# All low parts of the mixer's weights and rows on VectorE, between the HGRN levels

## The reference, cut to what matters

```
h = h + hybrid_mixer(rms_norm(h, norm1_g[layer]), w_in[layer], ..., w_out[layer], lb)
h = h + expert_choice_ffn(rms_norm(h, norm2_g[layer]), w_router[layer], ...)

def hybrid_mixer(xn, w_in, ret_g, hgrn_g, w_out, lb):
    proj = xn @ w_in                      # (256, 1024) @ (1024, 9*512)
    rq, rk, rv, rg, hq, hf_fwd, hf_bwd, hi, hg = jnp.split(proj, splits, axis=-1)
    r_out = retention, forward and backward, normalised, * silu(rg)
    h_out = HGRN2 scan, forward and backward, normalised, * silu(hg)
    return jnp.concatenate([r_out, h_out], axis=-1) @ w_out
```

## Time and profile before

| | |
|---|---|
| median of three runs | 2313.32 us |
| the profiled execution: span from first to last instruction | 2314.5 us |
| TensorE busy | 1928.7 us (83%) |
| VectorE busy | 816.0 us (35%) |
| ScalarE busy | 605.9 us (26%) |
| GpSimd busy | 170.2 us (7%), of that 120.7 us in 26 low halves |
| mean granted TensorE clock | 0.883 of full speed |

### The profile page before, as it was taken

One profiled execution on the slowest core, in us unless ns is written; L12 is line 12 of the kernel. 1 busy time (PEld: TensorE's weight loads), 2 busy tenths in 40 slices (PEclk: granted clock), 3 DMA queues, 4 the chain that ended last, 5 costly groups with the idle time before them and its releaser, 6 DMA issues.

```text
span 2314.5 us, 26791 instructions
## 1 busy us (share of the span) xinstructions
PE 1928.7 (83%) x10580; PEld 1227.7 (53%) x10580; DVE 816.0 (35%) x1196; ACT 605.9 (26%) x850; POOL 170.2 (7%) x70
## 2 busy tenths in 40 slices
PE   6897887777777789788767777766999999987998
PEld 5876532222232587654222222235888887445887
DVE  6566200000000556630000000046454455564776
ACT  5523211101111452312111111135222122253433
POOL 1333000000000132300000000021000000010000
PEclk9998887777777799888788888888999999998999
DMA  7373999999999636389999999941322224302551
GB/s 265 110 254 112 345 375 410 410 410 410 409 410 410 229 136 219 145 309 382 410 410 409 410 410 409 410 185 37 109 74 107 108 73 148 116 27 106 184 182 55
DMA packets 184534, 585.99 MB, mean 253 GB/s; under 512 B 6688, under 2 KB 7840, under 8 KB 184224
## 3 DMA queue, kind: packets, MB, share of 16 engines
q1 hardware_dynamic: 183152, 579.89, 65.0%
q0 software_dynamic: 896, 3.67, 0.4%
q10 hardware_dynamic: 432, 1.70, 0.2%
HBM read 584.19 MB, written 1.05 MB: 253 GB/s over the span
## 4 chain that ended last, share of the span: by engine, by line
PE 56%; DMA 17%; SPq 13%; DVE 7%; ACT 5%; issue 2%; POOL 1%; DVEq 0%; ACTq 0%; POOLq 0%
DMA ring<-in_w_down 16%; SPq L2189 11%; PE bank L461 10%; PE bank L463 10%; PE bank L462 10%; PE bank L791 3%; PE bank L778 3%; PE bank L809 3%; PE bank L819 3%; PE bank L940 2%; PE bank L619 2%; PE bank L473 2%; SPq L2195 2%; PE bank L1031 1%; ACT w_high L376 1%
## 5 line engine op out<-in xcount | busy, mean ns | idle before, releaser
L791 PE MATMUL bank<-ring,xeT 128*32 128x512 f32 x2048 | 280.9, 698 | 77.8 <-DMA ring<-in_w_up 58.7
L809 PE MATMUL bank<-ring,hid_T 128*32 128x512 f32 x1024 | 201.5, 930 | 81.2 <-DMA ring<-in_w_down 69.6
L791 PEld LDWEIGHTS bank<-ring,xeT 128*32 128x32 f32 x2048 | 69.3, 121 | 250.2 <-issue 160.5
L461 PE MATMUL bank<-x_high,w_high 128*128 128x512 f32 (+1 forms) x512 | 174.7, 341 | 17.0 <-DVE x_low L376 12.0
L376 POOL TENSOR_TENSOR w_low<-ring,w_high 128x2048 fp32r<-128x2048 f32 x26 | 120.7, 4643 | 821.6 <-ACT w_high L376 819.8
L463 PE MATMUL bank<-x_high,w_low 128*128 128x512 f32 (+1 forms) x512 | 175.4, 343 | 0.0
L462 PE MATMUL bank<-x_low,w_high 128*128 128x512 f32 (+1 forms) x512 | 173.7, 339 | 0.0
L1842 DVE TENSOR_TENSOR w_low<-ring,w_high 128x1024 fp32r<-128x1024 f32 x128 | 152.9, 1232 | 36.0 <-ACT w_high L1298 32.7
L1298 ACT ACTIVATE w_high<-ring 128x1024 fp32r<-128x1024 f32 x128 | 127.3, 1050 | 142.6 <-DMA ring<-in_w_mlp_in 64.0
L461 PE MATMUL bank<-w_high,hid_high 128*128 128x512 f32 x384 | 150.4, 392 | 0.0
L462 PE MATMUL bank<-w_low,hid_high 128*128 128x512 f32 x384 | 150.4, 392 | 0.0
(11 more groups left out here) (229 smaller groups left out, 2925.1 us busy)
## 6 DMA issues: line engine op xcount, KB each, us to landing
ring<-in_w_gate SPq DMA_DIRECT2D x128, 1024.0 KB, 18.5
ring<-in_w_up SPq DMA_DIRECT2D x128, 1024.0 KB, 18.6
ring<-in_w_down SPq DMA_DIRECT2D x64, 2048.0 KB, 22.4
ring<-in_w_ada SPq DMA_DIRECT2D x24, 2048.0 KB, 8.2
ring<-in_w_in SPq DMA_DIRECT2D x18, 2048.0 KB, 10.0
ring<-in_w_mlp_in SPq DMA_DIRECT2D x16, 2048.0 KB, 8.6
ring<-in_w_mlp_out SPq DMA_DIRECT2D x16, 2048.0 KB, 7.7
ring<-in_w_out SPq DMA_DIRECT2D x4, 2048.0 KB, 9.2
```

Of the source, the lines that this page charges most:

```text
L461: mm(ps, lh, rh, start=first, stop=False, skip_group_check=True)
L791: ins = mm(psum[4][32 * g:32 * g + 32, :], xeT[:, 2 * n + k, :], w[:, k, :, 256 * g:256 * (g + 1)], start=n == 0 and k == 0, stop=n == 3 a ...
L809: ins = mm(psum[5 + half][32 * g:32 * g + 32, :], hidT[:, n, 32 * g:32 * g + 32], w[:, g, half * 512:(half + 1) * 512], start=n == 0, stop ...
```

## The change

GpSimd forms no low part any more. VectorE forms all: the second half of item 0 and the two chunks of rows at the start of the layer in its own sequence, both halves of item 5 ahead of the HGRN levels, one half behind each of the first two units of RV (halves of item 6), HI (item 7), RG (item 8) and HG (item 9), and both halves of item 10 behind the last unit. The high parts on ScalarE are moved forward: item 7 from behind HI to behind the ADA ahead of it, item 8 from behind RG to behind the ADAs ahead of it, item 9 one ADA earlier, item 10 to just behind the last row tile of HG. The semaphores of the two engines become one. GpSimd keeps a memset, transfers, and its work in the second block.

```diff
--- before.py
+++ after.py
@@ -88,12 +88,7 @@
 
 
 SPLIT = [n for n, kind in enumerate(mixer_items()) if kind != ADA]
-SPLITS, BY_VECTOR = len(SPLIT) + 2, 5
-
-
-HALVES = [(j, half) for j in range(SPLITS) for half in range(2)]
-VECTOR_HALVES = [(j, half) for j, half in HALVES if j < BY_VECTOR and (j, half) != (0, 1)]
-POOL_HALVES = [x for x in HALVES if x not in VECTOR_HALVES]
+SPLITS = len(SPLIT) + 2
 
 
 def build_program(nc, x, cols, w_in, w_out, w_router, w_gate, w_up, w_down, final_g, ctx_x, w_ada,
@@ -390,16 +385,11 @@
 
             self.then_inc(read_by[name][0], 1, read_by[name][1])
 
-    def low_item(subtract, eng, l, j):
-
-        by, halves = (("split_by_pool", POOL_HALVES) if eng is nc.gpsimd
-                      else ("split_by_vector", VECTOR_HALVES))
-        for half in range(2):
-            if (j, half) not in halves:
-                continue
-            eng.wait_ge(S_("mix_high_ready"), 2 * (SPLITS * l + j) + half + 1)
-            whole, high, low = split_half(l, j, half)
-            subtract(low, whole, high.bitcast(F32), ALU.subtract).then_inc(S_(by), 1)
+    def low_half(subtract, eng, l, j, half):
+
+        eng.wait_ge(S_("mix_high_ready"), 2 * (SPLITS * l + j) + half + 1)
+        whole, high, low = split_half(l, j, half)
+        subtract(low, whole, high.bitcast(F32), ALU.subtract).then_inc(S_("mix_low_ready"), 1)
 
     def low_chunks(subtract, b):
 
@@ -500,18 +490,9 @@
 
                 if conversion is not None and c % 2 == 0:
                     b = c // 2
-                    if conversion:
-                        pe.wait_ge(S_("mix_x_split"), 6 * l + 2 + b + 1)
-                    elif b % 2 == 0:
-                        pe.wait_ge(S_("mix_x_split"), 6 * l + b // 2 + 1)
-                    else:
-                        pe.wait_ge(S_("mix_x_split_by_pool"), 2 * l + b // 2 + 1)
-                if c % 4:
-                    return
-                for by, halves in (("vector", VECTOR_HALVES), ("pool", POOL_HALVES)):
-                    if (j, c // 4) in halves:
-                        pe.wait_ge(S_("split_by_" + by),
-                                   len(halves) * l + halves.index((j, c // 4)) + 1)
+                    pe.wait_ge(S_("mix_x_split"), 8 * l + 4 * conversion + b + 1)
+                if c % 4 == 0:
+                    pe.wait_ge(S_("mix_low_ready"), 2 * (SPLITS * l + j) + c // 4 + 1)
 
             def split_parts(j):
 
@@ -1184,6 +1165,8 @@
                         ps = full(act, name)
                         func = ACT.Silu if kind in (RG, HG) else ACT.Copy
                         free(f(where[kind][:, t, :], ps[:, :], func), name)
+                        if (kind, t) == (HG, NT - 1):
+                            high_item(l, SPLITS - 1)
                         for _ in range(2):
                             if units[u][0] == P:
                                 name = ("unit", l, u)
@@ -1193,9 +1176,9 @@
                                        ACT.Copy), name)
                             u += 1
 
-                if n > 5 and n + 3 in SPLIT:
-                    high_item(l, SPLIT.index(n + 3))
-                if n == SPLIT[-1] - 1:
+                if n > 4 and n + 4 in SPLIT:
+                    high_item(l, SPLIT.index(n + 4))
+                if n + 4 == len(mixer_items()):
                     high_item(l, SPLITS - 2)
                 if kind == HG:
                     for t in range(NT):
@@ -1216,7 +1199,6 @@
             def mix_gain(c):
                 return C("ret_g", H4 * l + c) if c < H4 else C("hgrn_g", H4 * l + c - H4)
 
-            high_item(l, SPLITS - 1)
             high_chunks(("mix", l), mix_gain)
 
 
@@ -1474,9 +1456,9 @@
                         tick(ins)
                 free(ins, (tag, b))
 
-        def split_chunks(tag, gain):
-
-            for b in (0, 1, 2, 3) if tag[0] == "mix" else (0, 2):
+        def split_chunks(tag, gain, after=lambda b: None):
+
+            for b in range(4):
                 if b % 2 == 0:
                     ps = full(dve, (tag, b))
                     for c in (2 * b, 2 * b + 1):
@@ -1491,6 +1473,7 @@
                 else:
                     freed(dve, (tag, b))
                 low_chunks(tt, b).then_inc(S_("mix_x_split"), 1)
+                after(b)
 
         def lower_bounds():
 
@@ -1520,13 +1503,22 @@
 
         for l in range(DEPTH):
 
+            def low_item(j):
+                for half in range(2):
+                    low_half(tt, dve, l, j, half)
+
             for t in range(NT):
                 normalise(1, lambda _: h[:, t, :], lambda _: xs[:, t, :], "xs_ready", first=t)
-            low_item(tt, dve, l, 0)
+            low_half(tt, dve, l, 0, 0)
             if l == 0:
                 dve.wait_ge(S_("cols"), 16)
-            split_chunks(("x1", l), lambda c: C("norm1_g", KC * l + c))
-            low_item(tt, dve, l, 1)
+
+            def second_half(b):
+                if b == 1:
+                    low_half(tt, dve, l, 0, 1)
+
+            split_chunks(("x1", l), lambda c: C("norm1_g", KC * l + c), second_half)
+            low_item(1)
             if l == 0:
                 lower_bounds()
 
@@ -1550,8 +1542,9 @@
                     free(ins, name)
                     tt(rot[:, i, t, :], rope_t[:, 0, :], rope_t[:, 1, :],
                        ALU.add).then_inc(S_("rot_ready"), 1)
-                low_item(tt, dve, l, 2 + i)
-            low_item(tt, dve, l, 4)
+                low_item(2 + i)
+            low_item(4)
+            low_item(5)
 
             expect("forget_ready", 2)
             tt(hx[:, 0, :, :], hk[:, 0, :, :], hk[:, 1, :, :],
@@ -1648,17 +1641,22 @@
                 if 1 <= u <= 2 * len(LEVELS):
                     merge(u - 1)
 
+            next_item = 6
             for kind in mixer_items()[5:]:
                 if kind == ADA:
                     if ada_n:
                         ada_bias(ada_n - 1)
                     ada_n += 1
                 else:
-                    for _ in range(4):
+                    for part in range(4):
                         one_unit(u)
                         u += 1
+                        if part < 2:
+                            low_half(tt, dve, l, next_item, part)
+                    next_item += 1
                 if kind == HG:
 
+                    low_item(SPLITS - 1)
                     for t in range(NT):
                         expect("ret_sq_ready")
                         ins = reduce(rstat[:, 0, t, :],
@@ -2054,16 +2052,8 @@
         g.memset(eps[:, :], EPS).then_inc(S_("scattered"), 1)
         g.memset(cT[:, :, :], 0.0).then_inc(S_("ones_ready"), 1)
         for l in range(DEPTH):
-            low_item(turn(g.tensor_tensor), g, l, 0)
-            for b in (1, 3):
-                freed(pool, (("x1", l), b))
-                low_chunks(turn(g.tensor_tensor), b).then_inc(S_("mix_x_split_by_pool"), 1)
-            low_item(turn(g.tensor_tensor), g, l, BY_VECTOR)
-
             freed(pool, ("ret_s", l, H4 - 1))
             g.memset(kdec[:, :, :, :], 0.0).then_inc(S_("kdec_ready"), 1)
-            for j in range(BY_VECTOR + 1, SPLITS):
-                low_item(turn(g.tensor_tensor), g, l, j)
             freed(pool, ("w_out", l, 0, 0))
             g.dma_start(wr[:, :, :], w_router[l].rearrange("(c p) e -> p c e", p=P)).then_inc(
                 S_("router_landed"), 16)
```

## The result

The changed kernel takes 2343.51 us (median of 4 runs, 2335.95 to 2345.46); the kernel before took 2314.53 beside it (2312.31 to 2318.74). The ratio is 1.012, 95% interval 1.0099 to 1.014: it is slower by 29 us, where 12.4 had been forecast and 2334 was the upper end of the range.

A forecast was written before the change was run, and what follows sets the result against it. The prediction took TensorE's path through the two mixers as the bound, mixer delays lengthening the whole. Its terms summed to +6.2 us a layer, +12.4 for both: 2313.3 + 12.4 = 2325.7, say 2326 us, range 2314 to 2334.

The forecast's parts named there:

- Start and RV: Layer start to the end of the ADA behind RV: shorter VectorE instructions and TensorE waits, -0.2 and -5.9 us a layer.
- HI: Middle of HI: new 6.3 us TensorE wait for unit 5 behind the tile's landing, plus 2.7 us slow clock, +9.5 a layer.
- RG: Middle of RG, item 8: landing 8.9 us, TensorE wait 7.1 us, slow clock behind it, +10.3 us a layer.
- the bounds: Landing of 7.8 to 10.7 us instead of 8.1 and 8.9: -0.3 - 1.1 or +2.6 + 1.8 us a layer.
- HG: HG to the end of hgrn_out: 3.0 us wait before unit 13 without clock loss, stretched instructions gone, -3.9 us a layer.
- rival 3: HG's 3.0 us wait and the start's short wait also throttle: +2.7 and up to +1 us a layer, about 2332 us; chance 0.13.
- Normalisation: Normalisation: the second ret_gate falls from 4.33 to 0.69 us on the path to the transposes, -3.6 us a layer.
- Behind the mixers: Everything behind the second mixer: no change forecast, 0 us.
- Rival 2: Mixers: tiles there in time, HI and RG cost 0, only GpSimd's removal counts: -17 us a layer, 2279 us; chance 0.07.

The follow-up runs named there:

- second profile: The changed kernel run once more, unchanged: 2340.55 us, ratio 1.0111.
- filled waits: Changed kernel with extra matmuls nobody reads, worked off by TensorE before its waits for units 5, 9 and 13: 2332.74 us; on another bank 2327.4 us.
- 2283 and 2281: Changed kernel, low halves of items 7, 8, 9 behind third and fourth unit: 2282.75 us; that with item 10's high part behind hgrn_off: 2280.77 us.
- four kernels: Changed kernel, low halves later: items 7 to 9 behind fourth unit 2288.18 us, behind third and fourth 2282.75; only item 9 2321.45, only 7 and 8 2299.97.
- half tiles: Changed kernel loading only the first 512 of 1024 rows of RG's and HG's weight tiles: 2326.18 us, ratio 1.0059.
- subtraction and memset: Kernel with low halves behind third and fourth unit, plus one GpSimd subtraction in the normalisation: 2284.58 us; with two GpSimd memsets instead: 2282.44 us.
- the kernels of 2288 and 2283 us: Changed kernel with low halves of items 7, 8, 9 behind the fourth unit: 2288.18 us; behind the third and fourth unit: 2282.75 us.

## Why the prediction was wrong

The direction was right, and so was the mechanism of HI and RG; in HG the prediction left the clock out, and its sum was less than half of what was measured. By its own steps:

- *Start and RV*, -6.1: right, -5.4, though two misses partly cancel in it: the start gave about -0.7, not -0.2, and RV -4.7, not -5.9. The short wait keeps part of the gain back: behind the 2.10 us wait at 109.95 the clock was down and the ADA of RV took 3.6 us, not 1.92.
- *HI*, +9.5: right, +10.1. Landing 7.8 us for 8.1 taken, wait 6.18 for 6.3, unit 5 and the start of the row tile at half clock. (The 0.67 of the earlier trace rows for 110 to 111 is a mean: the clock was not "back at full" there but came back within that microsecond.)
- *RG*, +10.3: mechanism right, a term too small. "I take 8.9 us to landing": the transfer requested at 149.82 took 10.6 us and the wait was 8.91, not 7.1; in the second layer the wait was 7.89; +11.9. The end of the earlier trace rows that I kept for the bounds was the case in the first layer.
- *HG*, -3.9: this is the step that failed. "A wait of 3.0 us that I take as too short to let the clock fall": the wait was 2.81 and 3.58 us (2.70 and 3.54 in the second profile), but behind it the clock was at half. Stretches of the changed kernel in HG, first layer:

```profile
195.00:197.00 2.00, 0.00 (x0) 0.00 (x0) 1.93 (x3) 1.69 (x3) 0.00 (x0) 1.00 0.51 186
197.00:199.00 2.00, 1.62 (x8) 1.62 (x8) 1.83 (x4) 0.00 (x0) 0.00 (x0) 0.55 0.00 0
201.00:203.00 2.00, 2.00 (x6) 1.61 (x6) 1.93 (x3) 0.00 (x0) 0.00 (x0) 0.50 0.00 0
205.00:207.00 2.00, 2.00 (x10) 1.62 (x9) 0.71 (x2) 0.00 (x0) 0.00 (x0) 1.00 0.00 0
```

  The clock was still full in the idle 195 to 197 and fell (1.2 GHz) as unit 13 began: 0.55 over 197 to 199 leaves 0.2 us at full, and the unit began at 197.38. The unit took 3.4 us to the start of the row tile, and the row tile 6.9 to 8.0 in the four changed mixers, where 1.8 and 5.7 are full clock. It cost 3.3 us a layer by the filled waits. I had inferred the harmless 3.0 us from one row, the 2.08 us wait before unit 0, whose own unit ran at full clock but behind which the clock was already going down, as rival 3 said. With 3.3 us more in each layer the forecast would have been 2332 us; the changed kernel is still 8 to 11 us above that, by RG's landing (3 us in both layers), smaller misses in the other steps and, in the first profile, the 6.4 us behind the mixers. The part of rival 3 on HG was the true case, and its 2332 us had the same landing too short.
- *Normalisation*, -3.6: right, -3.6, and by the cause given: ret_gate is 0.69 us and the earlier trace rows had 4.33.
- *Behind the mixers*, 0: +6.4 in one profile, +0.1 in the other, the clock again. The range had no term for waits that move the clock where the change touches nothing.

The whole account of a layer, from the experiments: the waits themselves (with the 0.4 us before units 7 and 11) cost 7.9 (HI 26.3 - 18.4), 9.1 (RG 27.5 - 18.4) and 3.4 (HG 28.4 - 25.0), 20.4 us; the clock 8.3; given back are 5.4 up to A, 6.9 in HG (31.9 - 25.0), 3.6 and 0.6, 16.5 us. That leaves 12.2, against the 12.1 measured; the terms come from the same table, so it shows that nothing is missing, not that each is right. Rival 2 named what would have happened with the tiles there in time (-17 a layer, 2279 us): the kernels in which VectorE comes to the halves after they have landed reach 2283 and 2281.

Shown by experiments: the place in VectorE's order (four kernels), the landing (half tiles), the clock's share (filled waits), the contention (subtraction and memset). Only read from traces: that the 6.4 us are chance; no other profile has them, and nothing was changed to provoke it. Not known: what decides whether the clock falls behind a short wait. Not tried: loading the tiles earlier, into a slot of their own.

## What to carry to other kernels

An instruction taken over by another engine joins that engine's order: ask for each what it waits for and who stands behind it, more than how long it takes; here the low halves placed two units too early made the kernel 27 to 29 us slower than before, and two units later 32 us faster. An engine that was late enough to find its transfer landed hides the transfer's time; moved forward it waits, and whoever needs something that stands behind the wait pays. In the kernels of 2288 and 2283 us ScalarE waited as long, and TensorE paid nothing for it. Price a new TensorE wait as the wait plus a clock drop of about 3 us (2.6 to 4.0 here), unless a row shows work of the same kind staying at full clock behind a wait as long.

## What the runs showed of the hardware

Waits of 2.81 and 3.58 us of TensorE between units of narrow matmuls were followed by a granted clock of 0.50. In the second profile of the changed kernel so was one of 0.89 us (timeline of TensorE, first layer; the unit takes 3.39 us for 16 matmuls and the row tile behind it 7.5), where the first profile shows the same wait with a unit of 2.00 us and a row tile of 5.7:

```profile
98.53 3.39 PE L600 MATMUL bank<-qdec,hgrn_k 128*128 128x64 f32 x16 [0.89 <-DVE qdec L371]
```

The length of the last wait alone doesn't decide; with the same code the clock fell or did not. Keeping the clock gave back 2.2 to 3.3 us of a mixer for each drop.

A VectorE instruction of two SBUF inputs was held until about the end of GpSimd's reading instruction (2.23 us instead of 0.69), and not held at all by two GpSimd memsets that together took as long.
